# The next layer's norm, turns and page gathers inside the feed-forward down product; four of six search tiles on ScalarE; layers written out

## The chip, the core and the metric

The kernel runs on one core of one Trainium2 chip. The metric is the device time of one execution in microseconds (us), as a median over runs. The engines are TensorE (PE; PEld is its weight load), VectorE (DVE), ScalarE (ACT), GpSimd (POOL) and SyncE (SP); SPq and POOLq are the issues of DMAs on SP's and POOL's queues. Everything is float32.

## What is computed

The reference is one inference step of a two-layer hybrid decoder trunk over 1024 prompt rows and 64 sample rows (8 sequences of 8 tokens). Cut to what matters:

```python
for l in range(DEPTH):                                   # DEPTH = 2
    h = rmsnorm(x, norm_mix[l])                          # x (rows, 1024)
    pa, pb, pc = split_cols(h @ w_in[l], ...)            # one combined projection
    y_a = mlstm(pa)                                      # matrix memory
    y_b = sparse_attend(pb)                              # top 256 keys by index scores
    y_c = rwkv7(pc)                                      # time mixing
    x = x + concat(y_a, y_b, y_c) @ w_out[l]
    hf = rmsnorm(x, norm_ffn[l])
    x = x + (silu(hf @ w_gate[l]) * (hf @ w_up[l])) @ w_down[l]
y = rmsnorm(x, norm_final)
```

The index scores of a prompt row are taken against all earlier rows; those of a sample row also against 8192 cached keys, which lie in pages that a page table names. `top_k` is done as a search for a threshold, bit by bit.

## The kernel before

The 1088 rows (padded to 1152) are nine row tiles of 128, `TILES = NT + 1`, the last one with the 64 sample rows. One hardware loop over the layers (L3828) runs the stages one after the other, with a barrier of all engines between stages (`close_sems`):

- `stage_front` (L149): for each tile, load `x` from scratch memory, square it with a row sum (ACT L592), square root (ACT L594), reciprocal and scale (DVE L656, L657), turn it with 8 transposes (PE L467, `turn_in`) and copy the two PSUM halves into `nT` (DVE L662, ACT L599). Then 8 column chunks of `w_in` times 9 tiles: a *unit* is one chunk and one tile (PE L479; L477 for the sample tile). The first ten units are the nine of the narrow chunk `w_small` (80 columns) and the index queries of the sample tile, in the order sample-small, sample-queries, eight prompt-small. Unit results are rotated (DVE L674 to L679), turned (PE L519), copied to `tT` (DVE L699) and stored by SP (`store_turned`, L335). In program order behind the turned store of the third unit SP issues `load_index` (L346 to L354), 21 small loads. Beside the units POOL gathers the index-key pages of the layer in 16 pieces of 1 MB (L444), and writes each back to scratch memory in page order (L451); SP then loads them for the scores (L368). `idx` holds the indices for the gathers (DVE L705 to L709).
- `stage_attend_mix` and `stage_samples`: sample attention and the sample parts.
- `stage_prompt_mix` (L1745): two strands, `rwkv_strand` (time mixing of the prompt) and `dsa_strand` (L1353: index scores, search, exact threshold, pick, attention of the prompt). Both yield after each step, and `interleave` (L852) deals out the steps of the two in proportion to lists of planned costs, so that both strands end together; every engine walks the same order. In the search six row tiles with 384, 512, 640, 768, 896 and 1024 scores per row are counted against a candidate, in 32 rounds: the first `NDVE` of them on DVE (`count`, L1601), the other `NACT` on ACT (`sign`, L1527). Each round ends with three or four small DVE operations (`settle`, L1591 to L1596, and L1693), of which the last gives the next candidate `cand`. The tiles counted by ACT need three more DVE operations each afterwards (`recover`, L1608 to L1612).
- `stage_mix_ffn` (L3714): output projection with norm and turn (`stage_mix_out`), gate and up product (`ffn_up`), and `ffn_down` (L3620): for each tile 2 x 22 matmuls of 512 columns (PE L3669; L3677 for the samples), two adds to `x` (DVE L3697, L3704), and a store of `x` (SP L3645).
- After the loop `stage_final` (L3727) loads all nine tiles of `x` again, norms them and stores `y`.

Order on each engine is program order; waits are on semaphores.

## Time and profile before

| | us |
|---|---|
| median of 3 runs | 5890.93 (5890.17 to 5894.16) |
| the profiled execution, whole | 5880.55 |
| its span, first to last instruction | 5878.5 |
| PE busy | 4908.5 (83%) |
| DVE busy | 3002.9 (51%) |
| ACT busy | 1463.4 (25%) |
| POOL busy | 297.1 (5%) |

The profile is one execution. Times of its rows are microseconds from the start of the span. The median of the runs lies 10.4 us above the profiled execution, and that one 2.05 us above its span. In layer 1 the front stage lies at about 15 to 600 us, the prompt mix at 1141 to 1851, the down product at 2600 to 2924; in layer 2 the front stage lies at 2934 to 3560, the prompt mix at 4056 to 4765 and the down product ends at 5839. The final stage takes the rest. "Granted clock" (PEclk) is TensorE's clock as a share of 2.4 GHz.

### The profile page before, as it was taken

To read this page: it belongs to the slowest core of one execution; us is meant where nothing else is said; L and a number is where in the kernel's file an instruction comes from. 1 tells how busy PE (TensorE), PEld (TensorE's weight loads), DVE (VectorE), ACT (ScalarE), POOL (GpSimd) and SP (SyncE) were. 2 spreads that over 40 slices of the span, in tenths; PEclk is the share of its full clock that TensorE was granted. 3 is DMA by queue.
4 is the path that set the end of the run, shared out by engine and by line. 5 is a ranking of instruction groups with operands and counts; after the bars stand their busy time and mean duration, and the time that the engine had idled before them with its cause. 6 is when DMAs were issued, how large, how long until landed. Compare 5 with 4: busy or idle time off the path is not lost. (4 is left out here: it accounts for less than half of the span.)

```text
span 5878.5 us, 60639 instructions
## 1 busy us (share of the span) xinstructions
PE 4908.5 (83%) x22450; PEld 3137.8 (53%) x22474; DVE 3002.9 (51%) x6854; ACT 1463.4 (25%) x2742; POOL 297.1 (5%) x328
## 2 busy tenths in 40 slices
PE   5999675686698899999879996767667888999997
PEld 3344453455565588864343444435555655888543
DVE  2255454488774377740022645545887734777301
ACT  1242123356352100000022412332653511000000
POOL 1000232000000000000010003310000000000000
PEclk9999666575798999999989995665767999999998
DMA  8732333210002211122186324331100032111222
GB/s 292 237 109 80 110 99 101 60 30 17 17 20 110 104 61 65 66 82 64 60 293 189 112 78 118 110 95 38 38 9 22 15 116 112 52 66 66 88 68 102
DMA packets 376471, 524.63 MB, mean 89 GB/s; under 512 B 70210, under 2 KB 277636, under 8 KB 367524
## 3 DMA queue, kind: packets, MB, share of 16 engines
q1 hardware_dynamic: 329076, 381.31, 20.3%
q0 software_dynamic: 29696, 134.24, 7.1%
q10 hardware_dynamic: 17408, 5.25, 0.4%
q8 instruction: 178, 2.92, 0.2%
q14 instruction: 113, 0.93, 0.1%
HBM read 377.05 MB, written 153.80 MB: 90 GB/s over the span
## 5 line engine op out<-in xcount | busy, mean ns | idle before, releaser
L479 PE MATMUL pp<-w_in,nT 128*128 128x512 f32 x1792 | 802.6, 598 | 0.0
L479 PEld LDWEIGHTS pp<-w_in,nT 128*128 128x128 f32 x1792 | 329.8, 191 | 386.8 <-issue 386.7
L3492 PE MATMUL x<-nT,wgu 128*128 128x272 f32 x2112 | 509.7, 395 | 15.1 <-DMA wgu<-in_w_gate 15.1
L3669 PE MATMUL pm<-w_down,hT 128*128 128x512 f32 x1024 | 449.1, 597 | 27.7 <-DMA hT<-scratch_hT 27.7
L3492 PEld LDWEIGHTS x<-nT,wgu 128*128 128x128 f32 x2112 | 403.8, 191 | 99.8 <-DMA wgu<-in_w_gate 15.9
L3492 PE MATMUL x<-n_sum,w_sum 128*128 128x272 f32 x1408 | 342.0, 397 | 13.7 <-DVE n_sum L3551 13.7
L3669 PEld LDWEIGHTS pm<-w_down,hT 128*128 128x128 f32 x1024 | 196.0, 192 | 275.1 <-issue 275.1
L3697 DVE TENSOR_TENSOR x_tile<-pm,x_tile 128x512 f32<-128x512 f32 x32 | 22.1, 692 | 610.9 <-PE pm L3669 610.9
L3575 DVE RECIPROCAL exp_neg<-one_more 128x544 f32<-128x544 f32 x88 | 312.7, 3554 | 3.0
L1887 POOL DMA_INDIRECT kv_sel<-in_cache_kv,kv_idx x256 | 246.0, 961 | 1242.9 <-DVE kv_idx L2031 998.3
L3492 PEld LDWEIGHTS x<-n_sum,w_sum 128*128 128x128 f32 x1408 | 270.6, 192 | 71.0 <-issue 14.4
L1527 ACT ACTIVATE area<-score,cand 128x768 f32<-128x768 f32 (+2 forms) x192 | 198.1, 1033 | 129.6 <-DVE cand L1693 126.3
L699 DVE COPY tT<-p_turn 128x512 f32<-128x512 f32 (+2 forms) x72 | 37.7, 524 | 371.6 <-PE p_turn L519 334.4
L1898 PE MATMUL bank<-page_ranks,page_of_slot 64*128 64x130 f32 x512 | 138.0, 413 | 93.4 <-DVE slot_page L2023 74.6
L2022 DVE TENSOR_SCALAR_CACHE_REDUCE seen<-bank,c_slots 128x128 f32<-128x128 f32 x256 | 89.5, 349 | 220.0 <-PE bank L1898 140.4
L614 ACT ACTIVATE proj<-pp 128x512 f32<-128x512 f32 (+1 forms) x130 | 70.8, 544 | 475.7 <-PE pp L479 439.8
L1898 PEld LDWEIGHTS bank<-page_ranks,page_of_slot 64*128 64x128 f32 x512 | 105.4, 285 | 140.0 <-issue 139.8
L3522 ACT ACTIVATE exp_neg<-hT 128x544 f32<-128x544 f32 x88 | 57.8, 657 | 482.8 <-DVE hT L3556 292.0
L3669 PE MATMUL pm<-w_down_rest,hT 128*128 128x512 f32 x384 | 170.0, 592 | 0.0
L3492 PE MATMUL x<-nT,w_sum 128*128 128x272 f32 x704 | 168.5, 392 | 0.0
L3492 PE MATMUL x<-n_sum,wgu 128*128 128x272 f32 x704 | 168.5, 392 | 0.0
L3515 ACT ACTIVATE first_product<-x 128x544 f32<-128x544 f32 x44 | 27.4, 623 | 557.4 <-PE x L3492 557.4
(710 smaller groups left out, 8433.9 us busy)
## 6 DMA issues: line engine op xcount, KB each, us to landing
scratch_pages<-page_quarters POOLq DMA_DIRECT2D x32, 1024.0 KB, 8.5
area<-scratch_pages SPq DMA_DIRECT2D x64, 512.0 KB, 10.4
w_in<-in_w_in SPq DMA_DIRECT2D x14, 2048.0 KB, 8.9
scratch_hT<-hT SPq DMA_DIRECT2D x44, 544.0 KB, 2.9
wgu<-in_w_gate SPq DMA_DIRECT2D x22, 1024.0 KB, 5.4
wgu<-in_w_up SPq DMA_DIRECT2D x22, 1024.0 KB, 5.4
hT<-scratch_hT SPq DMA_DIRECT2D x16, 1408.0 KB, 7.4
w_down<-in_w_down SPq DMA_DIRECT2D x16, 1024.0 KB, 15.3
```

The source lines that it names most:

```text
L479: ins = pe.matmul(pp[u % 2][:, 0:cw], nT[:, k, t * P:(t + 1) * P], w[:, k, 0:cw], start=(k == 0), stop=(k == KT - 1))
L614: act.activation(pr[u % PR][:, 0:cw], pp[u % 2][:, 0:cw], ACT.Copy).then_inc(chunk_out, 1)
L699: dve.tensor_copy(tT[u % 2][:, 0:n, :], ptx[:, 0:n, :]).then_inc(turned_out, 1)
L1527: act.activation(rank[:, off[i]:off[i] + width(i)], acc[:, off[i]:off[i] + width(i)], ACT.Sign, bias=cand[:, n:n + 1].bitcast(F32), scale= ...
L1887: pool.indirect_dma_start(kv[n % RING][:, f, :], None, table, bass.IndirectOffsetOnAxis(ap=k_idx[:, token(n), f:f + 1], axis=0)).then_inc( ...
L1898: ins = pe.matmul(p_found[:, f, :], pick[n // 2 % 2][halves[n % 2], f * P:(f + 1) * P], rk[halves[n % 2], n // 2, :], start=True, stop=True)
L2022: chain(dve.tensor_scalar(seen[:, :], p_found[:, f, 0:PAGE], r1_col[:, f:f + 1], 0.0, ALU.is_lt, ALU.add, accum_out=off[:, token(n), f:f + ...
L3492: ins = pe.matmul(out[:, j, :], left[:, k, :], right[:, k, j * QN:(j + 1) * QN], start=(k == 0), stop=(k == HK - 1))
L3515: act.activation(p1[:, :, :], bank(M, P1), ACT.Copy).then_inc(p1_r, 1)
L3522: act.activation(e[n % 2][:, :, :], quarter(p, q), ACT.Exp, scale=-1.0).then_inc(exped, 1)
L3575: chain(dve.reciprocal(e[b][:, :, :], sg[:, :, :]))
L3669: ins = pe.matmul(pm[b][n][:, :], h[b][:, k, :], weights(k, slice(n * 512, (n + 1) * 512)), start=(k == 0), stop=(k == FT - 1))
```

## The change

Four things are changed.

1. `ffn_down` of layer 1 now also makes `nT` of layer 2: behind the adds of a tile ACT squares and takes the root, DVE scales, PE turns (`turn`, the tile before the one just multiplied), DVE and ACT copy into `nT`, which now outlives the stage. `stage_front` of layer 2 leaves all of this out, and its loads of `x`, `g` and `pages`; layer 1's front is as it was (`first`).
2. The 16 gathers of layer 2's index-key pages and their stores stand in `ffn_down` of layer 1, with two buffers in place of three.
3. `ffn_down` of layer 2 norms with `norm_final` and stores `y` itself, in place of storing `x`; `stage_final` is gone.
4. In the prompt's search `NDVE` is 2 in place of 3: four tiles on ACT. The list of planned costs of the search has four entries per round in place of three.

The loop over the layers is Python's, so the layer number is a constant in every instruction, and `ffn_down` has no loop of its own. Cut to its core:

```diff
@@ dsa_strand
-    NDVE = NTOP // 2
+    NDVE = NTOP // 3
     NACT = NTOP - NDVE
-    ROUNDS = (BITS + 1) * NDVE + 3 * NACT + 3 * NTOP
+    ROUNDS = (BITS + 1) * NACT + 3 * NACT + 3 * NTOP
...
         for r in range(BITS + 1):
-            for n in range(NDVE):
+            for n in range(NACT):
+                if n >= NDVE:
+                    yield
+                    continue
@@ stage_front, SP
-                load_x(0)
-                sp.dma_start(pages[:, :], io["pages"]).then_inc(pages_l, 16)
+                if first:
+                    load_x(0)
+                    sp.dma_start(pages[:, :], io["pages"]).then_inc(pages_l, 16)
...
+                if first:
+                    for o in range(1, TILES):
+                        load_x(o)
@@ stage_front, load_keys
-                    if J * per % P == 0:
+                    if first and J * per % P == 0:
                         for b in range(BUFS):
                             sp.wait_ge(put[b], 16 * puts_on(b, QUARTERS * (J * per // P + 1)))
@@ ffn_down, SP
+                for t in range(TILES):
+                    b = t % 2
+                    sp.wait_ge(x_new, 2 * t + 2)
+                    if not last:
+                        sp.dma_start(sc["x"][t * P:(t + 1) * P, :], x[b][:, :]).then_inc(stored[b], 16)
+                    sp.wait_ge(normed, t + 1)
+                    if last:
+                        sp.dma_start(out_rows(t), xn[b][0:P if t < NT else NS, :]).then_inc(y_stored[b], 16)
+                    else:
+                        sp.wait_ge(stored[b], 16 * (t // 2 + 1))
+                    if t + 2 < TILES:
+                        load(t + 2)
@@ ffn_down, POOL
+                if last:
+                    return
+                pool.wait_ge(idx_r, 1)
+                pool.wait_ge(rest_loaded, 16 * ((FT - W_AHEAD) // 2))
+                pool.wait_ge(h_loaded[1], 16)
+                for n in range(bufs - 1):
+                    gather(n)
+                for n in range(QUARTERS * GATHERS):
+                    put_out(n)
+                    if n + bufs - 1 < QUARTERS * GATHERS:
+                        gather(n + bufs - 1)
@@ ffn_down, PE
+                def turn(t):
+                    pe.wait_ge(normed, t + 1)
+                    pe.wait_ge(nT_ready, 2 * t)
+                    for k in range(KT):
+                        ins = pe.transpose(pt[k // 4][:, k % 4, :], xn[t % 2][:, k * P:(k + 1) * P], ident[:, :])
+                        if k % 4 == 3:
+                            ins.then_inc(nT_psum, 1)
...
+                for t in range(NT):
+                    step(t)
+                    if t and not last:
+                        turn(t - 1)
+                samples(NT)
+                if not last:
+                    turn(NT - 1)
+                    turn(NT)
@@ ffn_down, DVE (ACT the same with square and turned)
+                for t in range(TILES):
+                    add(t)
+                    norm(t)
+                    if t and not last:
+                        turned(t - 1)
+                if not last:
+                    turned(NT)
@@ build
-        with nc.Fori(0, DEPTH) as l:
-            stage_front(nc, l, io, sc, const)
+        with turned_rows() as nT:
+            stage_front(nc, 0, io, sc, const, nT)
+        for l in range(DEPTH):
...
+            with turned_rows() as nT:
+                stage_mix_ffn(nc, l, io, sc, const, nT)
+                if l + 1 < DEPTH:
+                    stage_front(nc, l + 1, io, sc, const, nT)
-        stage_final(nc, io, sc, const)
```

On PE the join of the layers was the end of `ffn_down`, the loop's branch, and (on the way round) the front stage from its top, which is the same for both layers:

```order
L3669 MATMUL pm_18844<-w_down,hT_18838 128x512 x16
L3669 MATMUL pm_18844<-w_down_rest,hT_18838 128x512 x6
L3677 MATMUL pm_18841<-w_down,hT_18837 64x512 x32
L3677 MATMUL pm_18841<-w_down_rest,hT_18837 64x512 x12
L3636 UNCONDITIONAL_BRANCH
L3828 REGISTER_ALU
L3828 COMPARE_AND_BRANCH
```

Now PE's rows there, the last prompt tile, the samples, the last turns, and the first units of layer 2's front, are these:

```order
L3739 MATMUL pm_18518<-w_down,hT_18508 128x512 x16
L3739 MATMUL pm_18518<-w_down_rest,hT_18508 128x512 x6
L3756 MATMUL pt_18519<-c_ident,xn_18511 128x128 x4
L3756 MATMUL pt_18520<-c_ident,xn_18511 128x128 x4
L3748 MATMUL pm_18515<-w_down,hT_18507 64x512 x32
L3748 MATMUL pm_18515<-w_down_rest,hT_18507 64x512 x12
L3756 MATMUL pt_18519<-c_ident,xn_18512 128x128 x4
L3756 MATMUL pt_18520<-c_ident,xn_18512 128x128 x4
L3756 MATMUL pt_18519<-c_ident,xn_18511 128x128 x4
L3756 MATMUL pt_18520<-c_ident,xn_18511 128x128 x4
L3670 UNCONDITIONAL_BRANCH
L474 UNCONDITIONAL_BRANCH
```

The turns of a tile stand behind the next tile's product, and the last two behind the samples.

On ACT in the search of the prompt mix, around the same four copies of the time-mixing strand (`tilde_T`), the rows were these before:

```order
L1527 ACTIVATE area,sign_sums<-score,cand 128x896
L1527 ACTIVATE area,sign_sums<-score,cand 128x1024
L1039 ACTIVATE tilde_T<-bank_8744 64x512
L1039 ACTIVATE tilde_T<-bank_8745 64x512
L1527 ACTIVATE area,sign_sums<-score,cand 128x768
L1039 ACTIVATE tilde_T<-bank_8746 64x512
L1039 ACTIVATE tilde_T<-bank_8743 64x512
L1527 ACTIVATE area,sign_sums<-score,cand 128x896
```

And with the change:

```order
L1541 ACTIVATE area,sign_sums<-score,cand 128x896
L1541 ACTIVATE area,sign_sums<-score,cand 128x1024
L1053 ACTIVATE tilde_T<-bank_8559 64x512
L1053 ACTIVATE tilde_T<-bank_8560 64x512
L1541 ACTIVATE area,sign_sums<-score,cand 128x640
L1053 ACTIVATE tilde_T<-bank_8561 64x512
L1053 ACTIVATE tilde_T<-bank_8558 64x512
L1541 ACTIVATE area,sign_sums<-score,cand 128x768
```

A round has a fourth tile on ACT, 640 wide, ahead of the other three.

## Rows read from the trace of the kernel before

**Rows 1.** Stretches of the span: busy us (and instructions) of each engine, granted clock, DMA.

```profile
core 0: us, PE busy (x) PEld busy (x) DVE busy (x) ACT busy (x) POOL busy (x), PEclk, DMA share, GB/s
1256.00:1457.00 201.00, 127.82 (x651) 109.29 (x654) 165.78 (x460) 131.40 (x256) 0.00 (x0) 0.58 0.09 24
1541.00:1851.00 310.00, 270.64 (x2166) 203.78 (x2173) 214.77 (x621) 151.63 (x328) 0.00 (x0) 0.91 0.04 16
2600.00:2925.00 325.00, 323.49 (x792) 140.70 (x792) 11.90 (x18) 0.00 (x0) 0.00 (x0) 0.99 0.22 70
3010.00:3560.00 550.00, 523.94 (x1745) 228.34 (x1744) 213.24 (x535) 149.44 (x216) 17.53 (x23) 0.96 0.48 150
```

**Rows 2.** Timeline of the end: start us, us, engine line op tiles.

```profile
5833.63 5.32 PE L3677 MATMUL pm<-w_down_rest,hT 128*64 128x512 f32 x24
...
5839.07 1.41 DVE L3704 TENSOR_TENSOR x_tile<-pm,x_tile 64x512 f32<-64x512 f32 x2 [18.42 <-PE pm L3677]
...
5845.29 5.99 SPq L3740 DMA_DIRECT2D x_all<-scratch_x  x9
...
5874.04 0.53 SPq L3745 DMA_DIRECT2D out_y_sample<-o_all  x1
```

**Rows 3.** Timeline of the join of the layers, ACT and DVE: one tile's norm.

```profile
2943.13 1.28 DVE L657 SCALAR_TENSOR_TENSOR xn<-s,stat,g_mix 128x1024 f32<-128x1024 f32 x1
...
2960.13 1.05 ACT L592 ACTIVATE xn<-area 128x1024 f32<-128x1024 f32 x1
...
2961.30 0.29 ACT L594 ACTIVATE stat<-stat,c_eps 128x1 f32<-128x1 f32 x1
```

**Rows 4.** Timeline of the join: PE, POOL and SP.

```profile
2918.71 5.32 PE L3677 MATMUL pm<-w_down_rest,hT 128*64 128x512 f32 x24
...
2930.56 0.34 POOL L434 MEMSET pick<- 128x288 f32 x1 [1961.06 <-POOLq L87]
...
2934.43 0.35 SPq L302 DMA_DIRECT2D s<-scratch_x  x1
...
2959.89 5.26 PE L477 MATMUL pp<-w_in,nT 128*64 128x256 f32 x32
2965.08 1.09 PE L467 MATMUL pt<-c_ident,xn 128*128 128x128 f32 x8
...
2982.10 3.60 SPq L349 DMA_DIRECT2D iq_all<-scratch_turned  x4
2985.74 16.22 SPq L354 DMA_DIRECT2D iw_cols<-scratch_iw  x16
...
3008.13 0.45 PE L519 MATMUL p_turn<-c_ident,q_pairs 128*128 128x128 f32 x1 [17.18 <-DVE tT L699]
```

**Rows 5.** DMA issues: tiles, queue, count, KB each, median us to landing.

```profile
scratch_pages<-page_quarters POOLq DMA_DIRECT2D x32, 1024.0 KB, 8.5
...
w_in<-in_w_in SPq DMA_DIRECT2D x14, 2048.0 KB, 8.9
...
hT<-scratch_hT SPq DMA_DIRECT2D x16, 1408.0 KB, 7.4
...
page_quarters<-in_cache_idx_kT,idx POOLq DMA_INDIRECT x32, 8.0
```

**Rows 6.** Timeline of the search, DVE and ACT: counts and signs.

```profile
1337.83 0.88 DVE L1601 TENSOR_SCALAR_CACHE_REDUCE area<-score,cand 128x640 f32<-128x640 f32 x1
...
1338.75 0.17 DVE L1243 TENSOR_SCALAR small<-small 128x4 f32<-128x4 f32 x1
...
1334.00 0.94 ACT L1527 ACTIVATE area<-score,cand 128x768 f32<-128x768 f32 x1 [0.18 <-DVE cand L1693]
...
1335.96 1.13 ACT L1527 ACTIVATE area<-score,cand 128x1024 f32<-128x1024 f32 x1
```

**Rows 7.** Groups by line in 1256 to 1457: busy us, mean ns | idle before.

```profile
L1601 DVE TENSOR_SCALAR_CACHE_REDUCE area<-score,cand 128x384 f32<-128x384 f32 (+2 forms) x96 | 71.4, 744 | 2.5
...
L1527 ACT ACTIVATE area<-score,cand 128x768 f32<-128x768 f32 (+2 forms) x96 | 99.0, 1033 | 64.1 <-DVE cand L1693 62.4 <-DVE cand L1695 1.6
```

## What the change does to the time: the prediction

> **What bounds the kernel now.** I read the busy time by stretches first, since the whole-span shares mix stages. The down product of layer 1 is PE alone: 323.5 of 325 us busy, DVE 11.9 and ACT nothing [rows 1]. The front stage behind its first 75 us is PE as well, 523.9 of 550 us [rows 1], so the gathers beside it cost nothing that I can find. The prompt's search is DVE's: 165.8 of 201 us, ACT 131.4, PE at a granted clock of 0.58; the attention behind it is nearer to PE, 270.6 of 310 us with DVE at 214.8 [rows 1]. Then I read the timeline at the two places where PE stands still: the end of the span [rows 2] and the join of the layers [rows 3, 4]. At the end, PE is done at 5838.95 and the span lasts 39.5 us longer. At the join, PE is done with layer 1 at 2924.03 and comes back to unbroken work only at 3008.13; between, it works on norms and small units and stands for 17.2 us behind SP. The sum is made against the profiled execution's span, 5878.5 us; the median of the runs is 12.4 us above that span, and I add that again at the end.
>
> **The end of the span: -30 us.** What is removed: the loads of nine tiles (SP starts at 5845.29), their squares, and the nine scalings. What is left behind the last add, which ends at 5840.48 [rows 2]: one square and root on ACT, 1.46 us from the square's start to the root's end; a reciprocal and one scaling of 1.28 on DVE, 1.45 together [rows 3]; two handoffs of about 0.1 us more; the last store, which from its issue at 5874.04 to the end of the span takes 4.46 us [rows 2]. 5840.48 + 1.46 + 1.45 + 0.2 + 4.46 = 5848.05, against 5878.5: -30.4. The stores of the other eight tiles lie under PE's 38 us per tile. I take -30; bounds -26 (a wait or two of 2 us more) and -32.
>
> **The join: -16 us.** PE's path first. Seven groups of turns now stand in PE's stream. One group of 8 is 1.09 us at full clock [rows 4], less its overlap with the next matmul about 0.95: +6.6, so the samples end at 2924.03 + 6.6 = 2930.6. Behind them: the add 1.41 [rows 2], the square and root 1.46, the scaling 1.45, turns 1.1, a copy of about 0.6, handoffs 0.4: 2937.0. The stage's barrier: before, the add ended about 1.5 us behind PE and POOL began the next stage at 2930.56, but SP only at 2934.43 [rows 4], so 3.9 us of the join are the way from the loop's branch to SP's first instruction. The trace doesn't name what that is; the end of the span has a barrier without such a branch, and there SP starts 4.8 us after the last add [rows 2], a store's landing among them. Now that store lands under the norm, so I take 2 us for the barrier alone (an estimate, between nothing and 4.8) and that the 3.9 us go with the branch: SP starts the front stage at 2937.0 + 2 = 2939. The Trainium skill (Runtime: NRT & Kernel Launch, section Instruction fetch mechanics) says that a taken branch whose target isn't in the fetched window stops the engine for a fetch of its page. By that rule the 3.9 us go; the row fits it without proving it, and the sum without it would be 4 us less gain.
>
> In the front stage, before, the second unit (sample queries) started at 2959.89, 25.5 us behind SP's start, since norms and turns came first; load_index was issued from 2982.10 at the latest and took SP until 3001.96, and PE resumed at 3008.13 [rows 4]. Now the second unit waits only for its 2 MB of `w_in`. That load is issued as SP's third, about 2.3 us in, and lands 8.9 us later in the median of its kind [rows 5]: 11.2, I take 12, since a second such load is right behind it. Bounds are 10 and 18 (a landing twice as long). From there to load_index: the unit 5.26, three small units with their rotations at about 2.5 each, and 1.5 to 2.5 for stores and semaphores: 15. So load_index starts at 2939 + 12 + 15 = 2966 and PE resumes 26 us later, 3008.13 - 2982.10, at 2992: -16. Which unit PE has reached by then is the same as before, because the wait is for `t_stored` of the same unit; so the 17 us stall stays, and is longer if anything. That is why the ten us of norms taken out of the front don't all come back at once: SP's 20 us of small loads are next late, and they are only begun earlier. Bounds: -6 and -20.
>
> **Gathers: 0.** POOL issued 16 gathers and 16 stores per layer, at landings of 8.0 and 8.5 us [rows 5]. With two buffers I reckon one gather with its store per 9 us, 145 us in all, inside 325. In the front stage their removal gives back nothing, by the 523.9 of 550 us. What they can cost is the load of `hT`: 7.4 us [rows 5], issued about 6 us after a tile's end, needed 38 us after it. Cover is 32 us, so it may take four times as long. The Trainium skill (DMA: Bandwidth & Descriptors, section Queues, rings and completion order) has each DMA engine take turns between the queues that have work. That speaks against moving gathers beside these loads: by it the 7.4 would become about 15, still inside the cover, and no run has shown it yet. I take 0, bound +15.
>
> **The search: -12 us per layer, -24 in both.** DVE loses 32 counts of 640 scores. One is 0.92 us from start to the next instruction's start [rows 6], so 29.4. ACT gains 32 signs of 640: the trace has 0.94 at 768 and 1.13 at 1024 [rows 6], so an estimate of 0.84, and 27 us. DVE also gets three more recover operations, about 2.5 us. But the plan changes too: the search's planned costs rise from 106.8 to 133.6 of a total that rises from 388.8 to 417.8, so it is dealt 32.0% of the time-mixing strand's 558 units of cost in place of 27.5%: 26 more units of 153, taken from the attention (about 18), the index scores and the pick.
> By DVE: 201 - 29.4, plus 26 units. The search's DVE time without counts (71.4 plus their reads of about 8) [rows 7] and without about 21 of settling is 65 us for 153 units, and the 35 us of idle DVE go with the same strand: 0.65 us per unit, 17 us. That gives 189. By ACT: 131.4 + 27 + 5 for the strand's share is 163; and in each round ACT must stand still while DVE settles, four dependent operations of 0.2 and two handoffs, 1.0 us: 32 more, 195. Before, ACT stood 64.1 us before its signs, 2.0 us per round [rows 7], of which 1.0 can't be used; the spare 1.0 is just what the new sign (0.84) and the strand's share (0.16) take. Two engines that near to each other never both run full, so I take 200 for the search, where it was 201. The gain comes outside it: the attention has 18 units less, at PE's rate of 127.8 us per 153 units at clock 0.58, or 0.53 at 0.91: -10; index scores and pick -5; recover +3. Sum -13, I take -12. Bounds: -27 (DVE's whole saving comes through) and +8.
>
> **Sum.** -30 - 16 + 0 - 24 = -70: a span of 5808.5, a median of 5890.9 - 70 = 5821. A kernel of this length can be told from no change at about 0.2%, 12 us.
>
> **Rivals.**
> *ACT takes the search over.* The rounds become ACT's, 6.5 us or so in place of 6.3, and eat what the plan gives elsewhere: the search change is worth 0. For it: ACT at 163 + 32 of 200. Against it: the units moved out of the attention are a gain whatever bounds the search. 5890.9 - 46 = 5845.
> *DVE's saving comes through whole.* DVE is the busier of the two before, 165.8 to 131.4 us [rows 1], so the stage may follow DVE's sum, -27 per layer: 5891 - 30 - 16 - 54 = 5791. Against it: the spare us of ACT is used up on average, so in half of the rounds it is overdrawn.
> *Gathers hold up the down product.* If `hT` lands later than 32 us, each of the four or so tiles under the gathers is late by some us, +15: 5836.
> *The change doesn't do what it says at the join.* `w_in` lands only after 18 us, and the 3.9 us are no matter of the branch: the join gives 6 in place of 16, 5831.
> *Slower than before.* The strands hang on each other: time mixing's copies on ACT (`tilde_T`, `Yl`) now stand behind four signs in place of three, PE waits for them at clock 0.58, DVE for PE, and the round grows instead of ACT's idle time shrinking. It costs 64 rounds x the growth of a round; the other gains are 46, plus 24 elsewhere in the mix, so it decides from 1.1 us per round on (6.3 to 7.4). With 1.4 us it is +90 - 70 = +20: 5911. For it: DVE is idle 35 us in the search with PE busy for 127.8 of 201, so the chain is already felt. Against it: a fourth sign is 0.84 us, and to lengthen each round by more than itself it would have to be in the chain twice.
>
> **Chances.** The forecast, 5805 to 5835: 0.47 (this takes in the case at the join). ACT takes over, 5835 to 5860: 0.25. DVE's saving whole, 5780 to 5805: 0.17. Gathers hold up: 0.07, mostly inside the ranges named. Slower than before or a wash: 0.04. The range for 8 in 10 reaches from 5788 to 5852. Faster by over 0.2% has 0.95, within 0.2% 0.02, slower 0.03.
>
> **What would show it.** Right: DVE's last scaling is one instruction, and the span ends about 9.5 us behind PE's last matmul; PE's samples of layer 1 are followed by 16 transposes and then, 25 to 30 us after the samples' end, by the sample queries' unit; PE again stands some 17 to 20 us behind `tT`, resuming about 16 us earlier than before; POOL's gathers end within 160 us of the down product's start, and PE has no wait for `hT` in tiles 2 to 7. In the prompt mix DVE's busy share of the search falls to under 0.75, ACT's rises over 0.8, the idle time before the signs falls from 2.0 to about 1.0 us per round, the search still lasts some 200 us and the attention some 10 us less. Wrong: a search of over 215 us or under 190; a wait of PE for `hT`; SP's start of the front later than 2942; a stall of PE in the front that is not behind load_index.

## The result, and the profile after

The changed kernel takes 5799.34 us in the median (5797.19 to 5804.15, 4 runs), against 5890.55 for the kernel before beside it: a ratio of 0.9845, with a 95% interval of 0.9828 to 0.9862. That is 91 us; the forecast was 70, to 5821. Between the two profiled executions the spans differ by 82.2 us, 5878.5 to 5796.3. The other 9 us are not in the traces: the profiled execution of before was a short one of its kind, 10 us under its median. The accounts below go by the spans.

| piece of the span (us) | before | after | moved | forecast |
|---|---|---|---|---|
| PE's last product to the end | 39.5 | 9.6 | -29.9 | -30 |
| start of layer 1's down product to PE's resumption behind `tT` | 407.6 | 377.4 | -30.2 | -16 |
| prompt mix of layer 1 / layer 2 | 705.6 / 707.7 | 695.7 / 694.7 | -22.9 | -24 |
| all else | | | +0.8 | 0 |

The prompt mix is taken from the first index product on PE to the start of DVE's last copy of the stage (`delta`). That all else comes to so little is in part luck: a second profile of the changed kernel (e12) is 20.6 us shorter, 15 of it in a stage that nobody touched.

**The end.** Timeline of the changed kernel, last 15 us: start us, us, engine line op tiles.

```profile
5781.40 5.32 PE L3748 MATMUL pm<-w_down_rest,hT 128*64 128x512 f32 x24
...
5786.84 1.41 DVE L3808 TENSOR_TENSOR x_tile<-pm,x_tile 64x512 f32<-64x512 f32 x2 [15.39 <-PE pm L3748]
5788.28 1.06 ACT L3779 ACTIVATE xn<-x_tile 128x1024 f32<-128x1024 f32 x1 [18.35 <-DVE x_tile L3808]
...
5789.46 0.30 ACT L3781 ACTIVATE stat<-stat,c_eps 128x1 f32<-128x1 f32 x1
...
5789.99 1.29 DVE L3813 SCALAR_TENSOR_TENSOR xn<-x_tile,stat,g_next 128x1024 f32<-128x1024 f32 x1
5791.35 0.51 SPq L3692 DMA_DIRECT2D out_y_sample<-xn  x1
```

One add, one square, one root, one scaling and one store stand where nine loads and nine norms stood [rows 2].

**The join.** Timeline of the changed kernel, PE, POOL and SP, between the layers (answers to [rows 4]).

```profile
2925.39 1.09 PE L3756 MATMUL pt<-c_ident,xn 128*128 128x128 f32 x8
2930.87 1.93 PE L3756 MATMUL pt<-c_ident,xn 128*128 128x128 f32 x8 [4.39 <-DVE nT L3817]
2939.27 3.70 PE L493 MATMUL pp<-w_small,nT 128*128 128x80 f32 x16 [6.46 <-DMA w_small<-in_w_in]
2945.57 6.51 PE L491 MATMUL pp<-w_in,nT 128*64 128x256 f32 x32 [2.60 <-DMA w_in<-in_w_in]
...
2973.49 0.45 PE L534 MATMUL p_turn<-c_ident,q_pairs 128*128 128x128 f32 x1 [8.00 <-DVE tT L717]
```

```profile
2935.61 0.34 POOL L447 MEMSET pick<- 128x288 f32 x1 [175.62 <-POOLq L87]
```

```profile
2935.60 0.38 SPq L407 DMA_DIRECT2D w_small<-in_w_in  x1
...
2961.46 2.70 SPq L359 DMA_DIRECT2D iq_all<-scratch_turned  x4
2964.20 5.74 SPq L364 DMA_DIRECT2D iw_cols<-scratch_iw  x16
```

POOL and SP now begin the stage together; before they lay 3.9 us apart. The row to look at is the last one: the same 16 small loads took SP 16.22 us before [rows 4] and take 5.74 now, and PE's stall behind `tT` falls from 17.18 to 8.00 us.

**Stretches.** The changed kernel: busy us (and instructions) of each engine, granted clock, DMA. The search, the attention of the prompt, the down product of layer 1 (answers to [rows 1]).

```profile
1259.00:1474.00 215.00, 135.74 (x722) 115.18 (x724) 150.96 (x419) 160.35 (x327) 0.00 (x0) 0.61 0.11 32
1557.00:1845.00 288.00, 252.25 (x2102) 186.34 (x2109) 207.46 (x610) 148.45 (x322) 0.00 (x0) 0.96 0.05 16
2596.00:2925.00 329.00, 328.92 (x848) 146.54 (x848) 27.70 (x46) 16.23 (x32) 24.61 (x32) 0.99 0.50 172
```

The down product has PE busy for 328.92 of 329 us, with the norms, the turns and POOL's 32 DMAs beside it. The search became longer (it was 199.4 us) and the attention much shorter (it was 317.7).

**Gathers.** POOL's first gather and last store in the down product, and the issues of `hT` over the whole kernel (count, KB each, median us to landing; before 7.4 [rows 5]).

```profile
2613.81 0.94 POOL L3707 DMA_INDIRECT page_quarters<-in_cache_idx_kT,idx  x1 [1637.88 <-DVE idx L142]
...
2759.41 0.57 POOL L3714 DMA_DIRECT2D scratch_pages<-page_quarters  x1 [7.84 <-DMA page_quarters<-in_cache_idx_kT,idx]
```

```profile
hT<-scratch_hT SPq DMA_DIRECT2D x16, 1408.0 KB, 8.1
```

The median of 16 hides what the gathers do, since only four of these loads were issued beside them. Those took 7.5, 7.5, 12.5 and 10.3 us (issued at 2642.46, 2680.32, 2720.84 and 2759.37), where the same four took 7.4 each before. All lie far inside the cover of 32 us.

**Search.** Groups by line of the changed kernel in 1259 to 1474 (busy us, mean ns | idle before), answers to [rows 7].

```profile
L1541 ACT ACTIVATE area<-score,cand 128x640 f32<-128x640 f32 (+1 forms) x126 | 122.9, 977 | 49.0 <-DVE cand L1710 46.3 <-DVE cand L1712 2.6
L1615 DVE TENSOR_SCALAR_CACHE_REDUCE area<-score,cand 128x384 f32<-128x384 f32 x64 | 43.4, 678 | 1.9
```

DVE's waits for ACT's counts in the search: us in total, times, longest. First the kernel before, then the changed one.

```profile
DVE counts L1591 <- ACT area L1527: 1.9, 3, 0.8
```

```profile
DVE counts L1605 <- ACT area L1541: 12.6, 11, 3.0
```

ACT still stands still for 49 us while DVE settles a round, and now DVE also stands for 12.6 us behind ACT: each waits for the other in turn.

### The profile page after: what moved, and what is told of

It reads as the page before. It is cut to its first block and busy times, and to the rows that moved or that the text cites. A ratio compares the mean times of both kernels' runs of the same rounds, so it can differ in the third digit from the quotient of the medians.

```text
span 5796.3 us, 59972 instructions
## 1 busy us (share of the span) xinstructions
PE 4906.6 (85%) x22450; PEld 3134.3 (54%) x22474; DVE 2954.7 (51%) x6746; ACT 1518.7 (26%) x2877; POOL 298.4 (5%) x328
## 5 line engine op out<-in xcount | busy, mean ns | idle before, releaser
L3509 PE MATMUL x<-n_sum,w_sum 128*128 128x272 f32 x1408 | 341.4, 396 | 12.6 <-DVE n_sum L3568 12.6
L3805 DVE TENSOR_TENSOR x_tile<-pm,x_tile 128x512 f32<-128x512 f32 x32 | 22.2, 693 | 538.2 <-PE pm L3739 538.2
L1541 ACT ACTIVATE area<-score,cand 128x640 f32<-128x640 f32 (+3 forms) x256 | 250.2, 979 | 97.6 <-DVE cand L1710 92.5
L3779 ACT ACTIVATE xn<-x_tile 128x1024 f32<-128x1024 f32 x18 | 19.0, 1057 | 693.1 <-DVE x_tile L3805 656.0
L3532 ACT ACTIVATE first_product<-x 128x544 f32<-128x544 f32 x44 | 27.5, 624 | 558.0 <-PE x L3509 558.0
```

Source lines behind the costliest of these rows:

```text
L1541: act.activation(rank[:, off[i]:off[i] + width(i)], acc[:, off[i]:off[i] + width(i)], ACT.Sign, bias=cand[:, n:n + 1].bitcast(F32), scale= ...
L3509: ins = pe.matmul(out[:, j, :], left[:, k, :], right[:, k, j * QN:(j + 1) * QN], start=(k == 0), stop=(k == HK - 1))
L3532: act.activation(p1[:, :, :], bank(M, P1), ACT.Copy).then_inc(p1_r, 1)
```

## The experiments

Twelve kernels ran in three groups of four, each group beside the kernel before, whose medians there were 5893.08, 5878.08 and 5875.52 us. Each group ran on another chip, so medians are compared inside a group, and across groups by their ratios against before of the same group. The first group, e1 to e4, asks what the gain in the prompt mix belongs to, the split of the tiles or the plan of costs that changed with it, and whether the gathers belong to the join.

### e1: three tiles each on DVE and ACT

```diff
-    NDVE = NTOP // 3
+    NDVE = NTOP // 2
```

The plan goes back with it, since its list has an entry for each tile on ACT.

> The changed kernel with the search as it was: three tiles on VectorE, three on ScalarE, and the planned costs that follow from that. Theory 1 (the search change is worth 10 to 13 us per layer, by the traces of before and after: prompt mix 705.6 to 695.7 and 707.7 to 694.7 us): the kernel is 23 us slower than the changed one, span about 5819, each prompt mix 706 us, the search 200 us (it was 214.5 in the changed kernel), the attention behind the picks 318 (288 in the changed one). Rival (part of the mix's gain comes from the layers being written out, not from the search): the mix stays under 702 us, the kernel is only 5 to 15 us slower.

Measured: 5828.54 us, ratio 0.9892 (0.9874 to 0.991), prompt mix 710.3 and 707.3 us.

### e2: the old split under the new plan

```diff
-    NDVE = NTOP // 3
+    NDVE = NTOP // 2
...
-        costs += [1.1 * width(i) / 1024 + 0.15 for i in TOPPED[NDVE:]]
+        costs += [(1.1 * width(i) / 1024 + 0.15) * 133.6 / 106.8 for i in TOPPED[NDVE:]]
```

> The changed kernel with three tiles on each engine as before, but with the search's planned costs scaled up so that their sum is the changed kernel's (133.6 for 106.8): only the dealing out of the time-mixing strand is new. Theory A (the mix gains by the fourth tile on ScalarE, which frees VectorE; the new plan alone only moves work): the search gets longer by the 26 units that it is dealt, at 0.65 us each, 200 to 217 us, and the attention shorter by 10 to 30: the mix about 700 to 706, the kernel 10 to 20 us slower than the changed one. Theory B (what gains is the plan: less time mixing in the attention, where TensorE is near its limit and its clock then rises earlier): the attention is 288 us as in the changed kernel, the search 217, the mix within 4 us of the changed kernel's 695, or better.

Measured: 5826.53 us, ratio 0.9892 (0.9875 to 0.9908), mix 702.6 and 713.8, mean 708.2.

### e3: the new split under the old plan

```diff
-        costs += [1.1 * width(i) / 1024 + 0.15 for i in TOPPED[NDVE:]]
+        costs += [(1.1 * width(i) / 1024 + 0.15) * 106.8 / 133.6 for i in TOPPED[NDVE:]]
```

> The changed kernel with four tiles on ScalarE, but with the search's planned costs scaled down so that their sum is what it was (106.8): only the split is new. Theory A (the split gains): VectorE is rid of 29 us of counts per layer and ScalarE has room, so the search falls to 185 to 192 us and the attention stays near 315; the mix 690 to 695 us. Theory B (the plan gains): ScalarE holds the round, the search is 197 to 202 us as before, the attention 315 to 318, the mix 703 to 708, and the kernel 15 to 25 us slower than the changed one.

Measured: 5801.36 us, ratio 0.9849 (0.9833 to 0.9866), mix 695.3 and 693.3.

With e8 below, this is the whole table, us in layer 1, layer 2. Search is DVE's first to last count; pick is from there to the last pick operation, with recover in it; attention is from there to the stage's last copy, each taken at the start of that last operation; all are times of operations in the traces.

| kernel | split DVE/ACT, planned cost | search | pick | attention | mix |
|---|---|---|---|---|---|
| before | 3/3, 106.8 | 199.4, 199.8 | 76.9, 75.5 | 317.7, 318.9 | 705.6, 707.7 |
| e1 | 3/3, 106.8 | 200.6, 199.6 | 77.1, 76.9 | 319.1, 317.3 | 710.3, 707.3 |
| e8 | 3/3, 120 | 213.2, 210.9 | 78.9, 80.5 | 306.0, 307.4 | 704.6, 706.6 |
| e2 | 3/3, 133.6 | 220.6, 223.1 | 73.1, 74.7 | 299.3, 302.2 | 702.6, 713.8 |
| e3 | 2/4, 106.8 | 204.6, 204.4 | 79.9, 80.5 | 299.1, 295.5 | 695.3, 693.3 |
| after | 2/4, 133.6 | 214.5, 214.2 | 83.3, 83.4 | 288.0, 287.6 | 695.7, 694.7 |

The split is worth 14.5 us per layer under the old plan (708.8 to 694.3) and 13.0 under the new (708.2 to 695.2). The plan is worth nothing that these runs can tell: -0.6 and +0.9, where the two layers of e2 alone lie 11.2 apart. The medians say the same of the split, 27 us for both layers between e1 and e3 of one group. The plan does move work, 10 and 22 us into the search and 10 and 17 out of the attention.

### e4: the gathers back in the front stage of layer 2

```diff
@@ ffn_down, POOL
-                if last:
-                    return
+                return
@@ stage_front, POOL
-                if not first:
-                    return
@@ load_keys
-                    if first and J * per % P == 0:
+                    if J * per % P == 0:
```

The load of `pages` and `place_indices` move back with them.

> The changed kernel with layer 2's 16 page gathers and their stores back beside the units of the front stage, with their pages and indices; the norm and the turns stay in the down product. Theory (gathers beside SP's 16 small loads of load_index stretch their issue: 16.2 us before, 5.7 in the changed kernel, where no gather runs): the 16 small loads take 14 to 18 us again, TensorE stands 15 to 19 us behind tT in place of 8, and the kernel is 8 to 12 us slower than the changed one. Rival (the loads of x tiles, 4.5 MB in the same queue, stretched them, and the gathers cost nothing, as the prediction had it): the small loads take 6 us, the stall is 8 us, the kernel within 2 us of the changed one.

Measured: 5817.81 us, ratio 0.9878 (0.9862 to 0.9895), span 5815.2, 19 us over the changed kernel's. Timeline at the join, SP and then PE:

```profile
2971.23 14.89 SPq L364 DMA_DIRECT2D iw_cols<-scratch_iw  x16
```

```profile
2991.60 0.45 PE L532 MATMUL p_turn<-c_ident,q_pairs 128*128 128x128 f32 x1 [16.00 <-DVE tT L715]
2995.40 5.06 PE L491 MATMUL pp<-w_in,nT 128*128 128x512 f32 x9
```

The down product starts at 2597.7 here, so PE resumes 393.9 us behind it: 407.6 before, 393.9 with norm and turns moved alone, 377.4 with the gathers moved too. The forecast of -16 was that of e4 (-13.7); the gathers' own -16.5 is what it had at zero. The loads of `x` aren't in this front stage, so it isn't they that stretch the 16 small ones. The 16.5 us are kept to the end of the stage: its last unit ends 904.9 us behind the start of the down product here, and 888.0 in the changed kernel.

### e5: e4 with the gathers held back

```diff
-                    pool.wait_ge(chunk_done, PAGES_AT + 5 * n // 4 + 1)
+                    pool.wait_ge(chunk_done, max(10, PAGES_AT + 5 * n // 4 + 1))
```

The gathers stay in both front stages, but the first five wait for the tenth unit, behind `load_index`.

> The kernel with layer 2's gathers back in the front stage (as in e4, 5818 us), but in both layers no gather starts before ten units are done, that is behind the 16 small loads of load_index. Theory (it is the traffic of the gathers at the same time that stretches SP's issues): the small loads take 6 to 7 us in both layers in place of 15 and about as much in layer 1, the stall of TensorE behind tT falls to 8 to 10 us in both, and the kernel takes 16 us less than e4 in layer 2 and 8 to 10 less in layer 1: about 5795. Rival (the gathers cost their time in the front wherever they lie, as traffic beside the other loads, or the pages then come too late for unit 14): the kernel stays at 5810 to 5820 and TensorE waits for the page pieces.

Measured: 5806.83 us, ratio 0.9869 (0.9852 to 0.9886). Layer 2, SP and then PE:

```profile
2956.10 5.75 SPq L364 DMA_DIRECT2D iw_cols<-scratch_iw  x16
```

```profile
2965.38 0.45 PE L532 MATMUL p_turn<-c_ident,q_pairs 128*128 128x128 f32 x1 [7.54 <-DVE tT L715]
3011.94 1.98 PE L547 MATMUL pi<-area,iq_rows 64*64 64x512 f32 x8 [9.62 <-DMA area<-scratch_pages]
```

The down product starts at 2588.4: PE resumes 377.0 us behind it, as in the changed kernel, and nothing differs from e4 but the moment of the gathers. This shows the cause: gathers and stores that run beside SP's small loads stretch them. Over the two front stages of all fourteen profiled executions, the 16 loads took 5.7 to 6.2 us in the 14 stages without a gather beside them and 7.6 to 20.6 in the 14 with gathers. Whether it is the gathers, the stores or their traffic was not tried. Nor do only POOL's DMAs do this: in the changed kernel one issue of `x_tile` behind SP's own load of `hT` and three of `w_down_rest` took 11.86 us (at 2594.18), before any gather.

The price is in the last row: PE now waits 15.9 us in all for pages. The front's last unit ends 908.2 us behind the start of the down product, against 904.9 in e4, so holding the gathers only trades one wait for another. Moving them out of the stage removes both.

### e6: the changed kernel with layer 1's gathers held the same way

The edit of e5, on the changed kernel; only layer 1 has gathers in its front.

> The changed kernel (5799 us), with the gathers of layer 1, which are still in the front stage, held back until ten units are done. Theory: layer 1's 16 small loads take about 6 us and its front stage is 8 to 12 us shorter: 5788 to 5791. Rival (in layer 1 the loads of x tiles keep SP's issues slow, or the pages come late): within 3 us of the changed kernel.

Measured: 5788.38 us, ratio 0.985 (0.9827 to 0.9873), span 5775.7. In layer 1 the 16 loads take 6.18 us in place of 16.93, and the stall behind `tT` 1.9 in place of 18.4. I first read the shorter span as the gain of this. It isn't: PE now waits 14.0 us for pages (8.8 and 5.2), and the front's last unit ends at 611.1, in the changed kernel at 608.4. e12 below settles it.

### e7: the kernel before with its loop written out

```diff
-        with nc.Fori(0, DEPTH) as l:
+        for l in range(DEPTH):
```

> The kernel before with the hardware loop over the layers replaced by two copies of its body, nothing else. Theory (3.9 us between the barrier and SP's first instruction of layer 2 are the way back through the loop's branch): SP starts layer 2's front 3 to 4 us earlier, and the kernel takes 3 to 5 us less than the kernel before. Rival 1 (those 3.9 us are the barrier's): no difference. Rival 2 (constants in place of registers in every DMA issue and wait save time all over): 10 us or more less.

Measured: 5867.39 us, ratio 0.9975 (0.9962 to 0.9989). At the join, POOL and then SP:

```profile
2929.10 0.34 POOL L434 MEMSET pick<- 128x288 f32 x1 [1963.29 <-POOLq L87]
```

```profile
2929.09 0.34 SPq L302 DMA_DIRECT2D s<-scratch_x  x1
...
2979.02 7.63 SPq L354 DMA_DIRECT2D iw_cols<-scratch_iw  x16
```

The 3.9 us between POOL and SP are gone, so they belonged to the loop. PE resumes 401.5 us behind the start of the down product in place of 407.6. This one join can account for some 6 of the 11 us between the medians; in the profile of e7 sample attention and the sample parts are 10 us shorter as well, which is inside their scatter (e12). The 16 loads took only 7.63 us here, with the gathers beside them, and yet PE stood for 16.4: SP's next eleven issues took 14.3 us (2986.70 to 3000.99), and 6.0 in before (3002.00 to 3008.01). The sums are alike, 21.9 and 22.2 us; where in SP's stream the stretching falls differs.

### e8: the old split under a plan between

```diff
-    NDVE = NTOP // 3
+    NDVE = NTOP // 2
...
+        costs += [(1.1 * width(i) / 1024 + 0.15) * 120.0 / 106.8 for i in TOPPED[NDVE:]]
```

> The changed kernel with three tiles on each engine and the search's planned costs halfway between old and new (120 for 106.8 and 133.6). With both of those plans the old split gave mixes of 707 to 708 us in the mean of the layers, the new split 694. Theory (the fourth tile on ScalarE is what gains, the plan is neutral): the mix is 704 to 711 us again and the kernel within 6 us of e1 and e2 (5826 to 5829). Rival (the mix depends by as much on how the two strands happen to meet, and the new split was lucky): with this plan the old split gives a mix under 700, or over 715.

Measured: 5820.22 us, ratio 0.9897 (0.9869 to 0.9925), mix 704.6 and 706.6 (the table). None of the three plans tried gives the old split what the new one has.

### e9: e1 with PE kept busy in the pick

The open question was why the split shortens the attention, in which no count stands. From e1 to e3 the planned cost of the search is the same, and PE does nearly the same matmuls in the attention (2196 and 2181), but in 299 us in place of 319. Stretches of the first 40 us of the attention, e1 and then e3; the granted clock stands behind POOL's `(x0)`.

```profile
1547.00:1587.00 40.00, 32.55 (x168) 27.36 (x169) 23.76 (x81) 13.41 (x42) 0.00 (x0) 0.63 0.00 1
```

```profile
1549.00:1589.00 40.00, 37.11 (x232) 29.19 (x230) 30.39 (x110) 18.40 (x56) 0.00 (x0) 0.79 0.02 7
```

The clock between TensorE's two levels (1.2 and 2.4 GHz) lies higher in e3. To try the clock alone:

```diff
@@ dsa_strand, PE
+        PICKING = 3 * NACT + 3 * NTOP
+        pe.wait_ge(idx_r, chunk0[-1])
         for n in range(ROUNDS):
+            for m in range(2 if n >= ROUNDS - PICKING else 0):
+                pe.matmul(bk[m % 2][:, :], ident[:, :], masks[:, 0:4, :], start=True, stop=True)
             yield
```

> The changed kernel with three search tiles each on DVE and ACT (as in e1), and beside the recover and pick steps of the search two extra PE products of 128x512 per step (54 in a layer), whose results nobody reads. Theory C: what the split of the tiles gives in the attention (319 us in e1, 299 in e3, same plan, same matmuls) is TensorE's granted clock, 0.63 in the first 40 us of e1's attention with a DVE-bound pick before it in which PE is busy 37.8 of 72 us. Then here the clock there is over 0.85, the attention takes 302 to 312 us in place of 319, and the mix 692 to 702 per layer in place of 708. Theory D: the clock is only a by-product, and the attention is as long as the chain of the strands makes it. Then the clock may rise, but the attention takes 316 to 322 and the mix 706 to 712, or more by what the extra products take (up to 10 us in the pick).

Measured: 5821.17 us, ratio 0.9902 (0.988 to 0.9924), mix 709.0 and 711.2. First 40 us of the attention:

```profile
1543.00:1583.00 40.00, 29.87 (x191) 23.59 (x190) 26.12 (x91) 14.77 (x46) 0.00 (x0) 0.82 0.00 1
```

The clock rose above that of e3, but the attention took 314.2 us, 5 less than e1 and 15 more than e3, and the pick gave the 5 back; in layer 2 the attention was 2 us under e1's. That lies between what C and D expected: the clock is the smaller part, at most a quarter of the 20 us, and C falls as an account of the gain. Measured from the end of the pick, the first output tile of the attention is copied after 44.7 us in e1, 41.1 in e9, 33.0 in e3: 12 of the 20 us are there in the first of eight tiles. What differs there is the order. PE of e1, and then of e3, at the end of the pick:

```profile
1547.73 1.92 PE L1139 MATMUL bank<-c_ident,tilde 128*64 128x128 f32 x8 [2.06 <-DVE tilde L1274]
1550.33 3.56 PE L1094 MATMUL bank<-tilde_T 64*128 64x128 f32 x15 [0.68 <-ACT tilde_T L1053]
1553.48 0.58 PE L1474 MATMUL bank<-kT,qT 64*128 64x128 f32 x1
```

```profile
1543.49 3.62 PE L1139 MATMUL bank<-c_ident,tilde 128*64 128x128 f32 x16 [13.40 <-DVE tilde L1271]
1547.79 4.45 PE L1094 MATMUL bank<-tilde_T 64*128 64x128 f32 x31 [0.68 <-ACT tilde_T L1053]
1551.83 0.58 PE L1474 MATMUL bank<-kT,qT 64*128 64x128 f32 x1
```

When the attention's first score (L1474) comes, e3 has 31 of the time mixing's `tilde_T` products behind it and e1 has 15. With four entries per round in place of three the strands are dealt out a few steps otherwise, though the search's planned cost is equal. That this difference of order makes the gain is read from the traces and wasn't tried: three tiles on DVE with four entries per round would have told it. So what the table calls the split is two things, the fourth tile on ACT and the fourth entry per round.

### e10: the changed kernel with PE kept busy in search and pick

The same edit on the changed kernel, with 1 in place of 0 for the rounds of the search.

> The changed kernel (two tiles on DVE, four on ACT) with extra PE products of 128x512 whose results nobody reads: one per step of the search's rounds (128 in a layer) and two per step of recover and pick (60). By theory C the granted clock, 0.61 in the search and 0.59 in recover and pick, rises to 0.9 or more from the pick on, and the first 20 us of the attention (0.79) as well: the mix gains 4 to 10 us per layer by shorter PE chains, median 5780 to 5792. If the search is held by ACT and DVE alone, its own length stays within 3 us of 214. By theory D the mix is 695 or longer: the extra products are in PE's order before the other strand's, up to 0.9 us each at the low clock, and the search grows by 10 us or more, median 5815 to 5840.

Measured: 5828.16 us, ratio 0.9914 (0.9893 to 0.9935). Stretches of search and attention:

```profile
1247.00:1466.00 219.00, 200.40 (x984) 124.27 (x983) 150.08 (x418) 160.46 (x326) 0.00 (x0) 0.96 0.11 31
...
1564.00:1849.00 285.00, 252.35 (x2106) 185.51 (x2106) 207.12 (x610) 147.99 (x322) 0.00 (x0) 0.96 0.05 17
```

The clock in the search went from 0.61 to 0.96, and the search still took 218.6 us, 4 more. The pick took 15 more. So filling PE doesn't pay. It doesn't show that the low clock costs nothing: the extra products stand in PE's order before those of the other strand (PE busy for 200 of 219 us, before 136 of 215) and may have cost what the clock gave.

### e11: e6 with the page scores two units later

```diff
-    START, RATE = 14, 2
+    START, RATE = (16 if first else 14), 2
```

> The changed kernel with layer 1's gathers held until the first ten units are done (as in e6), and the page scores of layer 1 begun two units later (16 in place of 14). In e6 PE waited 8.8 and 5.2 us for pages. If the lateness is all there is to those waits, the two units (14 us) hide them, layer 1's front is 10 to 14 us shorter than in e6 if the search behind it isn't made longer by its later start, or as long as e6's if the time is given back at the end of the front; median 5775 to 5790, against the changed kernel's 5797 to 5801 in the same job.

Measured: 5795.52 us, ratio 0.9845 (0.9823 to 0.9867), span 5798.1. The last unit of layer 1's front ends at 613.6. Groups of PE in layer 1's front from 100 us on, first both groups of page scores of e11, then the first of the changed kernel (e12), whose second has no wait either; idle us before them stand at the end.

```profile
L549 PE MATMUL pi<-area,iq_rows 64*64 64x512 f32 x128 | 18.3, 644 | 7.5 <-DMA area<-scratch_pages 7.5
L549 PE MATMUL pt<-area,iq_rows 64*64 64x512 f32 x128 | 17.4, 614 | 2.7 <-DMA area<-scratch_pages 2.7
```

```profile
L549 PE MATMUL pi<-area,iq_rows 64*64 64x512 f32 x128 | 17.4, 614 | 0.0
```

PE resumed at 84.0 us in place of 97.9, but waits 10.2 for pages and 4.7 behind `tT` later: the 14 are given back within the stage. That the two units would hide the lateness was wrong; the pages are paced by the gathers.

### e12: the changed kernel once more

> The changed kernel itself, once more, beside e10 and e11: 5795 to 5805, the span 5794 to 5800. Its stages should agree with the first profile within 2 us (search 214.5, attention 288, join 381).

Measured: 5786.22 us (5777.86 to 5802.12), ratio 0.985 (0.9829 to 0.987), span 5775.7, the same as e6's and 20.6 under the first profile's. The search took 216.0, the attention 288.1, and PE resumed at the join 375.7 us behind the start of the down product (377.4 in the first profile). Where do 20 us go in the same kernel? 15 of them into one stage: from the last unit of the front to the first index product, sample attention and the sample parts, it took 530.6 and 531.1 us in place of 540.7 and 536.3, and the mix of layer 2 took 4 less. Over all fourteen profiled executions, of before, of the change and of every experiment, that stage takes 524 to 543 us per layer with no kernel of them touching it, while the changed kernel's two executions agree within 4 us in every other stage. Some of this may go with the chip: the stage's mean is 539 us over the profiles of the first group, 531 of the second and 534 of the third, and the medians of before differ in the same direction (5893, 5878, 5876). It isn't more than a hint, since there is one profile per kernel, and the spread inside the second group alone is 15 us. So e6 gained nothing over the changed kernel, and no version here beats it: e6, e11, e12 and e3 have ratios from 0.9845 to 0.985.

## Why the prediction was right, and where it was not

The measured median, 5799, lies inside the range for 8 in 10 (5788 to 5852), but outside the forecast's own stretch of 5805 to 5835. It fell where the prediction had put the rival "DVE's saving comes through whole" (5780 to 5805), and not for that rival's reason: the mix gave 22.9 us and not 54. The missing 14 us are in the join, the other 9 are those by which the medians moved more than the profiled executions.

**The end** was right to half a microsecond in 30: square and root took 1.48 us (1.46 forecast) and the scaling 1.29 (1.28). The half is the last store, 4.95 us from its issue to the end of the span in place of 4.46.

**The join** was right in its chain and wrong in its last link. Counted from the start of the down product, SP's start was forecast at 338.5 and came at 339.5; the sample queries at 350.5 and 349.5; `load_index` at 365.5 and 365.4 (L359). Then 26 us to the resumption, taken from before; it was 12.0. The sentence that failed is "so the 17 us stall stays, and is longer if anything". It took the 16.22 us of `iw_cols` as SP's own cost, though a single issue of SP is 0.35 us there (L302, [rows 4]), and 16 of those are 5.6. The row was a contended one, and the change took its contender away. e5 shows it with the gathers left in the stage and only moved in time. Two of the signs named failed here: PE was to stand 17 to 20 us behind `tT` and stood 8.0. The sample queries were to start 25 to 30 us behind the samples' end and started 20 behind it, as the prediction's own sum had it (2951 against 2930.6).

**The branch.** The 3.9 us were taken as the loop's, and e7 confirms it. The rule of the Trainium skill (Runtime: NRT & Kernel Launch, section Instruction fetch mechanics), that a taken branch out of the fetched window costs a fetch, agrees with 3.9 us gone; no run shows the fetch itself.

**Gathers: 0** was right for the down product, where PE has no wait for `hT` behind its start, the pieces took 146 us (145 forecast) and `hT` landed in at most 12.5 us beside them, 7.4 without. It was wrong by -16.5 for the front stage. The argument was that PE was busy for 523.9 of 550 us there; that stretch begins at 3010, just behind the stall, and so leaves out the place where the gathers hurt. The rival that they hold up the down product fell. The Trainium skill's other rule, that each DMA engine takes turns between the queues that have work (DMA: Bandwidth & Descriptors, section Queues, rings and completion order), gave the prediction an estimate of 15 us for `hT`. Of the four loads beside POOL's pieces two took 7.5 us, as good as alone, and two 12.5 and 10.3, so the estimate lay above all four; the traces don't show the turns themselves.

**The search** has the right size, 22.9 against 24, by luck: the reasons were wrong. The search was to stay at 200 us and took 214.5; the attention was to give 10 per layer and gave 30; idle time before the signs was to fall to 1.0 us per round and fell from 2.0 to 1.5 (49.0 by 32). ACT's busy share was to rise over 0.8 and is 0.75 (160.35 of 215.00); DVE's is 0.70, under the 0.75 forecast. A search of over 215 us was named as a sign of being wrong: it took 214.5 in the first profile and 216.0 in the second. The failed step is the credit given to the plan: "the gain comes outside it", through units taken from the attention. The plan moves such units (PE does 722 matmuls in the search in place of 651), but e1 against e2 and e3 against after give it 0 within a microsecond in the mean of the layers. The split, with the fourth entry per round that came with it, has all of it, 13 to 14.5 per layer. The prediction reckoned with 26 units more in the search; 32.0% less 27.5% of 558 are 25, which changes nothing here. Nor does it come where its work is: with DVE freed of some 29 us in the search (32 counts), the search is 4 us longer in e3 than in e1. Neither rival of the search describes this: ACT didn't take over, since it stands still for 49 us, and DVE's saving didn't come through. Why the split shortens the attention stays open: e9 leaves the clock a quarter of it at most, and the order of the strands was not tried.

**The sum.** Only the join was mis-sized: -70 with -30 in place of -16 there is -84, and the spans moved by 82. The chain to a slower kernel was seen in part: the round grew from 6.2 to 6.7 us, and DVE's waits for ACT's counts from 1.9 to 12.6 us over the search. In e3, under the old plan, the round is 6.4. That stayed under the 1.1 us per round from which the rival reckoned a loss, and the link that it named, PE's waits for ACT's `Yl`, shrank from 20.3 to 13.6 us.

## What to carry to other kernels

Before a long row is taken as an engine's own cost, divide it by its count and compare it with the cheapest row of the same kind: 16.22 us for 16 loads beside 0.35 for one points to contention, and whatever moves the contender moves the row. Then follow the gain to the end of the stage: holding the contender back gave the row its 10 us and the stage none. When a change alters both the work and the list that orders it, run the four combinations; the size of a gain can agree while its reason doesn't. And repeat the kernel itself beside any variant that seems to win by 10 us: here one stage that nobody had touched scatters by as much, and the groups ran on different chips.

## What the runs showed of the chip

- Beside POOL's gathers and stores of 1 MB the issue of 16 small loads of SP took 7.6 to 20.6 us in place of 5.7 to 6.2, while the landing of a 1.4 MB load of `hT` grew from 7.4 to at most 12.5 us.
- Filling PE with unread products raised the granted clock from 0.61 to 0.96 over the search, and no stage that was filled got shorter: search 214.5 to 218.6 us, pick 83 to 98.
- Sample attention and the sample parts vary from 524 to 543 us between executions with the same instructions. Part of it may go with the chip; no run here tells why.
